# Context rows summed by TensorE beside the latents' heads, and the two layers of the first block in one program block

## The reference

```
first_block, for each of 2 layers l:
    h = rmsnorm(x, norm_mix[l]);  proj = h @ w_in[l]
    x = x + concat(mlstm, moba, nsa)(proj) @ w_out[l]
    h = rmsnorm(x, norm_ffn[l])
    x = x + square(relu(h @ w_ff1[l])) @ w_ff2[l]

second_block, latents x (256 tokens) and context xc (256 tokens), for i in 0, 1:
    attention of x over keys and values of x and xc;  x = x + g1 * (o @ w_o[i])
    the same for xc over its own keys (only i = 0)
    x = x + g2 * peer_ffn(h2, ...);   xc = xc + cg2 * peer_ffn(h2c, ...)  (only i = 0)

peer_block:  for each token 8 heads x 16 experts out of 16384 are picked:
    act = gelu(sum_d u_tab[expert] * h)          (a dot product with a gathered row u)
    out = sum over the 128 picks of g * act * v_tab[expert]   (a weighted sum of gathered rows v)
```

## Time and profile before

| | |
|---|---|
| median of 3 runs | 3413.68 us (3407.22 to 3416.61) |
| profiled execution, its own time | 3419.62 us |
| its span | 3417.8 us |
| PE / PEld / DVE / ACT / POOL busy | 2513.3 / 1409.4 / 2169.2 / 457.4 / 1318.3 us |
| HBM read | 1040.23 MB, 305 GB/s over the span |
| mean granted TensorE clock | 0.859 |

### The profile page before, as it was taken

One profiled execution on the slowest core, in us unless ns is written; L12 is line 12 of the kernel. 1 busy time (PEld: TensorE's weight loads), 2 busy tenths in 40 slices (PEclk: granted clock), 3 DMA queues, 4 the chain that ended last, 5 costly groups with the idle time before them and its releaser, 6 DMA issues. The chain is left out here.

```text
span 3417.8 us, 25077 instructions
## 1 busy us (share of the span) xinstructions
PE 2513.3 (74%) x7868; PEld 1409.4 (41%) x7868; DVE 2169.2 (63%) x5160; ACT 457.4 (13%) x1350; POOL 1318.3 (39%) x1084
## 2 busy tenths in 40 slices
PE   5786196599959469972567888887866768888876
PEld 2343154377345448431434333343333433333332
DVE  1439745856656766657867767777526377777774
ACT  0210011100002100000111111111112111111111
POOL 0000023645634555634734445454300054444442
PEclk8888597599979579986678999999988889999998
DMA  6655264789977689977858999999850199999996
GB/s 252 250 201 196 85 233 154 271 330 393 349 260 258 217 281 390 391 297 285 277 166 330 419 417 419 419 421 421 372 195 25 43 401 419 419 419 421 421 421 286
DMA packets 248920, 1044.63 MB, mean 306 GB/s; under 512 B 20518, under 2 KB 53398, under 8 KB 176852
## 3 DMA queue, kind: packets, MB, share of 16 engines
q0 software_dynamic: 147456, 805.37, 59.6%
q1 hardware_dynamic: 93584, 222.23, 17.6%
q10 hardware_dynamic: 7748, 15.43, 1.3%
HBM read 1040.23 MB, written 2.72 MB: 305 GB/s over the span
## 5 line engine op out<-in xcount | busy, mean ns | idle before, releaser
L1173 POOL DMA_INDIRECT sb_beside_slots<-in_peer_uv,sb_beside_chosen x512 | 591.6, 1156 | 616.9 <-issue 308.5
L1146 DVE SCALAR_TENSOR_TENSOR sb_beside_slots<-sb_beside_slots,sb_beside_H 128x1024 f32<-128x1024 f32 x256 | 312.7, 1223 | 236.9 <-DMA sb_beside_slots<-in_peer_uv,sb_beside_chosen 234.9
L1165 DVE SCALAR_TENSOR_TENSOR sb_xc<-sb_beside_slots,sb_beside_small,sb_xc 128x1024 f32<-128x1024 f32 x254 | 325.6, 1282 | 3.5 <-DMA sb_beside_slots<-in_peer_uv,sb_beside_chosen 1.5
L174 PE MATMUL psum<-sb_f_arena,sb_f_ring 128*128 128x256 f32 (+1 forms) x1344 | 297.6, 385 | 5.5 <-issue 5.5
L174 PEld LDWEIGHTS psum<-sb_f_arena,sb_f_ring 128*128 128x128 f32 (+1 forms) x1344 | 252.8, 189 | 50.1 <-issue 7.6
L174 PE MATMUL psum<-sb_f_ring,sb_f_arena 128*128 128x512 f32 (+2 forms) x448 | 195.6, 599 | 5.7 <-DVE sb_f_arena L1672 5.7
L1079 PE MATMUL psum<-sb_latents_ring,sb_latents_scores 128*128 128x512 f32 x304 | 147.8, 638 | 48.4 <-ACT sb_latents_scores L1037 48.4
L1079 PE MATMUL psum<-sb_last_ring,sb_last_scores 128*128 128x512 f32 x276 | 135.5, 640 | 51.2 <-ACT sb_last_scores L1037 51.2
L1079 PE MATMUL psum<-sb_beside_slots,sb_latents_scores 128*128 128x512 f32 x288 | 145.2, 652 | 30.8 <-ACT sb_latents_scores L1037 30.8
L1915 PE MATMUL psum<-sb_f_ring,sb_f_arena 128*128 128x512 f32 x384 | 165.1, 592 | 0.0
L935 POOL DMA_INDIRECT sb_latents_ring<-in_peer_uv,sb_latents_scores x76 | 91.9, 1209 | 127.1 <-PE psum L1079 86.8
(11 more groups left out here) (494 smaller groups left out, 4738.4 us busy)
## 6 DMA issues: line engine op xcount, KB each, us to landing
sb_f_ring<-in_w_ff SPq DMA_DIRECT2D x32, 2048.0 KB, 12.8
sb_context_ring<-in_ada_w SPq DMA_DIRECT2D x24, 2048.0 KB, 9.5
sb_f_ring<-in_w_in SPq DMA_DIRECT2D x8, 2048.0 KB, 12.8
sb_f_ring<-in_w_in SPq DMA_DIRECT2D x6, 1904.0 KB, 17.3
sb_context_ring<-in_peer_w_q SPq DMA_DIRECT2D x8, 1024.0 KB, 7.8
sb_beside_slots<-in_peer_uv,sb_beside_chosen POOLq DMA_INDIRECT x512, 6.4
sb_f_ring<-in_w_out SPq DMA_DIRECT2D x4, 2048.0 KB, 8.0
sb_latents_ring<-in_peer_w_q SPq DMA_DIRECT2D x8, 1024.0 KB, 25.4
```

What stands on the lines that cost most here:

```text
L174: last = e.matmul(out, a, b, start=(i == 0), stop=(i == len(terms) - 1))
L1146: e.scalar_tensor_tensor(out=self.u_slot[s % 4], in0=self.u_slot[s % 4], scalar=1.0, in1=self.H[:, s // (PH * TOPK), :], op0=ALU.mult, op1 ...
L1165: e.scalar_tensor_tensor(out=acc, in0=row, scalar=wn, in1=acc, op0=ALU.mult, op1=ALU.add).then_inc(self.added, 1)
L1173: return e.indirect_dma_start(out=to, out_offset=None, in_=self.table, in_offset=bass.IndirectOffsetOnAxis(ap=at, axis=0), element_offset= ...
```

## The change

Five things are changed together.

1. In the latents' head loop the rows n = 200 to 245 are no longer added by VectorE. ScalarE writes a diagonal of each row's weight (a 128x128 copy of the identity with the weight as scale), and TensorE multiplies it with the gathered row into two spare PSUM banks (two matmuls of 512 columns). `added` is counted up by TensorE for these rows. There are four diagonals. VectorE adds the two banks to `xc` behind the head loop, and TensorE waits for that (`joined`) before it transposes the heads' outputs.
2. Ten of the 22 steps ahead of the heads move into the head loop: 12 are left, and turns 4 to 13 of the loop take 3 steps, the others 2.
3. The two layers of the first block become one program block: one order of PSUM tiles, one weight ring that runs on, no barrier and no clearing between them. The parameters of layer 1 are loaded during the feed-forward part of layer 0 and turned between its chunks 2 and 3.
4. x is put into the feed-forward accumulator by TensorE (four matmuls with the identity), and ScalarE takes square and copy of the finished banks straight from PSUM. Layer 0's last chunk is ordered by token tile.
5. At the start of both layers ScalarE does what VectorE did: the copies of `cols`, the normalized rows (two of 128x1024) and the copies of the transposed rows (sixteen of 128x128 in place of two of 128x1024). GpSimd computes mean square and root itself, for layer 1 behind the gathers up to step 97.

```
+    beside_rows = [3 if 4 <= i < 14 else 2 for i in range(n_heads + 2)]
+    early_rows = 12
+    if beside:
+        beside.give_to_tensor(beside.at_vector + early_rows - Beside.LAG, sum(beside_rows))
...
     def scalar(e):
...
                 e.activation(pbuf[(i - 1) % 3][2][:, 0:nk], st.pair(("p", i - 1))[:, 0, 0:nk], ACT.Copy).then_inc(*st.empties(("p", i - 1)))
+            if beside:
+                beside.scalar(e, sb["weighed"], beside_rows[i])
...
     def vector(e):
...
-        more(22)
+        more(early_rows)
...
         for i in range(n_heads + 2):
-            more(2)
+            more(beside_rows[i])
...
+        if beside:
+            beside.summed(e, beside_banks)
...
     def tensor(e):
...
                 matmuls(e, st.pair(("o", j))[:, 0, 0:HD2], [...]).then_inc(st.mm, 1)
+            if beside:
+                beside.tensor(e, sb["weighed"], beside_banks, beside_rows[i])
...
+        if beside:
+            e.wait_ge(beside.joined, 2)

 class Beside, vector():
-            if n >= 0:
+            if n >= 0 and not self.on_tensor[0] <= n < self.on_tensor[1]:
...
+    def scalar(self, e, diag, rows):
+        for n in range(self.n_diag, min(self.n_diag + rows, self.on_tensor[1])):
+            e.wait_ge(self.w_ready, n // ROWS + 1)
+            if n >= self.on_tensor[0] + 4:
+                e.wait_ge(self.added, n - 3)
+            e.activation(diag[:, n % 4, :], self.C("ident"), ACT.Copy, scale=...w(n)...).then_inc(self.diag_ready, 1)
...
+    def tensor(self, e, diag, banks, rows):
+        first, end = self.on_tensor
+        for n in range(self.n_summed, min(self.n_summed + rows, end)):
+            e.wait_ge(self.diag_ready, n - first + 1)
+            e.wait_ge(self.v_in[n % 4], 16 * (n // 4 + 1))
+            for half in range(2):
+                done = e.matmul(banks[half], diag[:, n % 4, :], self.v_slot[n % 4][:, half * 512:(half + 1) * 512], start=(n == first), stop=(n == end - 1))
+            done.then_inc(self.added, 1)

 first_block, scalar():
+        for t in range(NT):
+            if gone:
+                e.wait_ge(*gone.st.computed(accs[t]))
+                e.activation(by_bank(hn, t), gone.st.pair(accs[t])[:, :, :], ACT.Square, accum_out=ss1[:, t:t + 1]).then_inc(sumsq, 1)
+                e.activation(by_bank(x, t), gone.st.pair(accs[t])[:, :, :], ACT.Copy).then_inc(*gone.st.empties(accs[t]))
...
+            e.activation(hn[:, t, :], x[:, t, :], ACT.Copy, scale=rs1[:, t:t + 1]).then_inc(hn_ready, 1)
...
+            for k in range(KT):
+                done = e.activation(hT[:, k, t * P:(t + 1) * P], turned[:, k, :], ACT.Copy, scale=cols[:, k, 4:5])
 first_block, vector():
-        beside.vector(e, 28 if l == 0 else 18)
-        e.wait_ge(ff2_done, 8)
-        for t, acc in enumerate(("accA", "accB")):
-            e.tensor_tensor(xv, xv, st.pair(acc)[:, :, :], ALU.add)
+        beside.vector(e, 18)
+        if not last:
+            beside.mark((l + 1, 0))
+            beside.vector(e, 10)
 first_block, gpsimd():
+        beside.gpsimd(e, beside.marks[l, 0] + 1 if gone else 0)
+        for t in range(NT):
+            e.wait_ge(sumsq, t + 1)
+            e.tensor_scalar(rs1[:, t:t + 1], ss1[:, t:t + 1], 1.0 / D, EPS, ALU.mult, ALU.add).then_inc(pool_step, 1)
+            e.wait_ge(pool_step, t + 1)
+            e.tensor_tensor(rs1[:, t:t + 1], rs1[:, t:t + 1], C("m05")[:, 0:1], ALU.pow).then_inc(rstd, 1)
 first_block, tensor():
+        for t in range(NT):
+            for half in range(2):
+                e.matmul(acc[t][:, half, :], ident, x[:, t, half * 512:(half + 1) * 512], start=True, stop=False)
...
+            if c == 3 and not last:
+                blocks[l + 1].column_group(e)
```

More of the change, by code:

```diff
@@ L398, in scalar @@
             e.wait_ge(y_ready, n_y)
-        for i in range(n_heads + 1):
+        for i in range(n_heads + 2):
             if i < n_heads:
@@ L1166, in vector, with give_to_tensor, summed @@
         self.at_vector = min(self.at_vector + steps, self.STEPS)
+    def give_to_tensor(self, first, count):
+        self.on_tensor = (first, first + count)
+        self.n_diag = self.n_summed = first
+    def scalar(self, e, diag, rows):
[3 more added lines that the diff above has]
+                e.wait_ge(self.added, n - 3)
+            e.activation(diag[:, n % 4, :], self.C("ident"), ACT.Copy, scale=self.buf(n // ROWS)[4][:, n % ROWS:n % ROWS + 1]).then_inc(self.diag_ready, 1)
+        self.n_diag = min(self.n_diag + rows, self.on_tensor[1])
+    def tensor(self, e, diag, banks, rows):
[6 more added lines that the diff above has]
+            done.then_inc(self.added, 1)
+        self.n_summed = min(self.n_summed + rows, end)
+    def summed(self, e, banks):
+        end = self.on_tensor[1]
+        acc = self.acc[(end - 1) // (PH * TOPK)]
+        e.wait_ge(self.added, end)
+        for half in range(2):
+            cols = slice(half * 512, (half + 1) * 512)
+            e.tensor_tensor(acc[:, cols], acc[:, cols], banks[half], ALU.add).then_inc(self.joined, 1)
+        e.wait_ge(self.joined, 2)
     def mark(self, name):
@@ L1679, in vector @@
             e.wait_ge(*st.emptied(("wo", c)))
-        norm_to_T(ss2, rs2, 2, "fT", 5)
+        e.wait_ge(sumsq, 2 * NT)
+        rms_rows(e, rs2, ss2, D).then_inc(var, 1)
+        beside.mark((l, 5))
+        e.wait_ge(rstd, 7)
+        for t in range(NT):
+            e.tensor_scalar(hn[:, t, :], x[:, t, :], rs2[:, t:t + 1], None, ALU.mult).then_inc(hn_ready, 1)
+        for t in range(NT):
+            e.wait_ge(*st.computed(("fT", t)))
+            e.tensor_tensor(hT[:, :, t * P:(t + 1) * P], flat(st.pair(("fT", t)), "p b (k n) -> p (b k) n", k=4), wide(cols[:, :, 5:6], [P, KT, P]), ALU.mult).then_inc(*st.empties(("fT", t)))
         for c in range(8):
@@ L1704, in claim @@
             return st.pair(name)
-        e.wait_ge(par, 160)
-        ps = claim("cols")
-        pc = ps[:, 0, 0:64].rearrange("p (k r) -> p k r", r=8)
-        for k in range(KT):
-            n = 7 if k < 4 else 6
-            flip(e, pc[:, k, 0:n], rows[0:n, k * P:(k + 1) * P], ident)
-        flip(e, ps[:, 0, 64:96], pe_rows[0:32, :], ident).then_inc(st.mm, 1)
+        if not gone:
+            column_group(e)
         def turned(name, turn):
@@ L1955, in layer_memory @@
     sb["slots"] = slots
+    sb["weighed"] = None if last else mem("weighed", [P, 4, P])
     return sb
@@ L2009, in build @@
                 sb = first_memory(mem(inner, "f_"))
[L2010 to L2011 removed]
+                first_blocks(nc, sems, psum, sb, A, C, x, beside)
             with ExitStack() as whole:
```

192 lines of the change are left out of this document (134 added, 58 removed).

## The result

The changed kernel takes 3547.43 us (median, 3543.86 to 3549.58); the kernel before, run beside it, takes 3413.22 us. The ratio is 1.0394, 95% interval 1.038 to 1.0408. The forecast was 3482 us, slower by 68.8; measured are 134 slower, outside its range. The profiled execution took 3549.58 us (span 3546.9), 129.96 more than that of before.

The account below looks back on a forecast made before the run. VectorE paces the head loop, its dots waiting on a chain of sums and gathers. 3419.62 + 129 - 33.6 - 30 + 3 + 0.4 = 3488.4, or +68.8; on the median, 3482.5 us, range 3425 to 3535.

Parts of the forecast that it names:

- Direction and mechanism of the loop: Head loop: gathers wait for sums behind each turn's maximum, so the loop grows by 129 us to 252.
- the upper bound: Head loop with landing 5.8, gathers at 1.5, low clock: 20.3 and 14 us a turn, 296 us, +172.
- Part 2: Ahead of the heads: ten steps fewer let the squares of q and k start earlier, gain 33.6 us.
- Part 1, the sum of a row: Head loop: a row's two matmuls on TensorE cost 0.59 + 0.43 us, 1.4 with diagonal and hand-overs at today's clock.
- R + 3.9: Head loop: R is the start of a turn's maximum; the first v gather was put 3.9 us behind it.
- rival (b): Head loop: TensorE falls to its low clock, every sum takes 1.9 us; 3510 to 3530 us, chance 12%.
- Part 1, the landing: Head loop: a turn's third u row lands 5.0 us after issue, since fewer bytes are under way.
- Parts 3 to 5, from layer 0 to layer 1: First block: projections 38.6 us earlier, VectorE 21 plus its 12.3 us wait; gain 30 us, bounds 18 to 38.
- The -26.6 of the table: Stretch up to the latents' first squares on ScalarE: forecast difference -26.6 us.
- Parts 3 to 5, the start of layer 0: Layer 0's start: ScalarE's copies and scaling lengthen TensorE's chain by 3 us, bounds 0 to 5.
- Rival (a), bound by issue: Head loop bound by GpSimd's issue, not the chain: loop 142 us, kernel 3373 us; chance 10%.
- Rival (c): First block gives back its gain, steps and weights meeting on DMA engines, VectorE setting layer 1's end: 3512 us, 8%.

Follow-up runs that it names:

- Experiments 1 and 2: Changed kernel with diagonals made ahead of the exponentials, 3422.68 us; changed kernel with v gathers issued two rows later from the loop's first step, 3451.29 us.
- experiment 6: Changed kernel with TensorE summing only each row's left half, 3521.13 us; the same also fetching only the left half of those v rows, 3503.32 us.
- experiment 5: Changed kernel's timeline between the layers read; then joined blocks with the old head part, GpSimd issuing four more rows before layer 1's roots: 3388.1 us.
- experiment 4: Changed kernel with the head part of the kernel before (VectorE adds all rows, 22 steps early, 2 a turn): 3401.69 us, ratio 0.9945.
- Experiment 1: Changed kernel with one edit, ScalarE making each turn's diagonals ahead of the exponentials and their wait for the maximum: 3422.68 us, ratio 1.0009.

## Why the prediction was wrong

Two steps carry the miss: a row's sum and a row's landing were priced too low in the head loop (38 us), and a gain of 30 us between the layers was booked that did not come (17 us of it missing).

- **Direction and mechanism of the loop: right.** The head loop is the place, and the circle sum, v gather, u gather, dot, maximum, exponentials, diagonal is what it waits for. Experiments 1 and 2 cut it at two different links, and 125 and 96 us vanish. The turns are those of the upper bound (20.3 and 14 us a turn, 296 in all; measured 20.2, 13.7 and 290), not those of the forecast. The loop alone would have given some 3520 us, inside the range; the missing gain of the first block took the time out of it.
- **Part 2: right.** 33.6 us forecast, 33.6 measured (L540 at 1552.73, right behind the third copy's end).
- **Part 1, the sum of a row: the mis-sized term.** I priced a row at two matmuls, 0.59 and 0.43, and put the first v gather at R + 3.9. It is issued at R + 5.89 in the turn shown and at R + 6.1 in the mean of turns 5 to 13. The profile's groups show four records a row, not two (184 for the 46 rows, 92 with half sums; and in the experts' stage, which the change leaves alone and whose counts the profile of before has too, 304 for 76 rows):

```profile
L1201 PE MATMUL psum<-sb_beside_slots,sb_latents_weighed 128*128 128x512 f32 x184 | 113.3, 777 | 131.8 <-ACT sb_latents_weighed L1192 131.7
L1093 PE MATMUL psum<-sb_latents_ring,sb_latents_scores 128*128 128x512 f32 x304 | 152.6, 655 | 52.1 <-ACT sb_latents_scores L1051 52.1
...
L949 POOL DMA_INDIRECT sb_latents_ring<-in_peer_uv,sb_latents_scores x76 | 92.5, 1217 | 129.8 <-PE psum L1093 89.5
```

  I took one instruction for one pass. Besides, the first row meets the low clock: its weight loads are 0.85 us apart and from 1668.4 on 0.43. In these two stretches of the turn the granted clock is 0.50 and 1.00 (columns as in the windows above):

```profile
1664.10:1668.20 4.10, 4.04 (x5) 1.85 (x6) 0.00 (x0) 0.59 (x3) 0.00 (x0) 0.50 0.02 6
1668.20:1671.00 2.80, 2.80 (x8) 1.16 (x7) 0.00 (x0) 0.00 (x0) 2.18 (x3) 1.00 0.36 83
```

  That was rival (b) in part. Half a sum less gave 1.7 us a turn back (experiment 6).
- **Part 1, the landing: the second such term.** 5.0 forecast, 5.3 for the first and 6.04 for the third u row of the turn shown. I argued that fewer bytes are under way; in the mean that holds (149 GB/s), but within a burst of six gathers it doesn't. Experiment 6 shows the bytes in it. By the rule of the Trainium skill that the forecast weighed (SBUF — State Buffer, "The DMA setup-cost knee") it would have been an estimated 3.2 us; the trace, with 5.26 to 6.09, disagrees more than I had it.
- Together: 2.9 us in each of nine turns of three steps (26), 2.0 in three turns of two (6), 4.5 in the two transitions and 2.4 in turn 15, less some 0.5 at the two ends, make the 38 us by which 290.3 exceeds 252. Of the 2.9, the sum is 2.2 and the landing 0.9, less 0.3 on the gathers and power operations between them.
- **Parts 3 to 5, from layer 0 to layer 1: the failed step.** The starts came as forecast (projections 945.1 for 946.5, dot of step 98 at 944.0 for 943.5, convolution 977.9 for 974). What failed is the step from VectorE's 12.3 us at L1467 to a gain of 12 us there: I took them for time by which TensorE was late, and so for time that an earlier start of the projections would give back. The projection that VectorE waits for stands behind a product of VectorE's own scan, as TensorE's 21.8 us wait for L1594 and the rows of experiment 5 show; only 1.5 us of it were TensorE's lateness, and the wait stayed at 12.6. The gain was therefore VectorE's 17 us alone (I had 21 for it), and some 8 of it ran out on the way: 17.2 at the convolution, 18.9 at the product L1917, 17.2 again at L1611, 11.8 at the addition of the output projection, 10.5 at the end of the second feed-forward product. Two pieces are traced. The product takes 3.75 us in place of 1.99, at a granted clock of 0.50 behind TensorE's long stop where it was 1.00 before. And the four matmuls of x take 3.4 us (eight records, the same error) in place of the 1.7 that the forecast had. The rest stays open. The -26.6 of the table became -9.4 in this execution and -15 in the medians of experiment 4; the bounds for this gain, 18 to 38 us, did not hold it.
- **Parts 3 to 5, the start of layer 0:** 3 us forecast, 0.7 measured. From the turning of the parameter rows to the projections it is 9.05 us (421.31 to 430.36) against 8.34 in the earlier trace rows; the turning itself comes 0.8 later because in this execution the whole stage starts 2.6 us later. Sixteen copies take 4.23 us, 0.26 each, not 0.39. The Trainium skill's estimate of 0.25 us for 128 columns from PSUM (VectorE: DVE Perf Modes, TRN2 errata) fits the trace better than my row from SBUF.
- **Rival (a), bound by issue:** it was described as what happens when the sums of a turn come ahead of its maximum. Experiment 1 is that kernel, and its loop is 164.7 us and not 142. Rival (c), the first block gives all back, did not happen in full: a third to a half of the 30 us was left. But its statement that VectorE sets layer 1 is what experiment 5 showed; whether rows and weights meet on the DMA engines there was not tested. Of the total of +61 us over the forecast in the profiled executions, the loop is 38, the first block 17 and the rest of the span 5.

## What to carry to other kernels

Before an operation is moved to an idle engine, write down what stands ahead of it in that engine's stream, and who waits for its result; here 59 us of VectorE's work was saved and the loop grew by 167 us, and one call, moved from the end of the loop's body to its start, took 125 of it back. Count a matmul's price from the records of the trace per unit of work, not from instructions in the source. And before a wait is booked as a gain, above all one whose releaser the profile calls "issue", read what ends it in the other engines' rows and follow that back: here it led to the waiting engine itself.

## What the runs showed of the hardware

- A float32 matmul instruction of 128x512 leaves two records, 0.43 us apart at the full clock and 0.85 at the low one (184 records for 92 instructions, 92 for the 46 of the half sums); so a row of 1024 columns costs 1.7 us on TensorE at the full clock where VectorE's addition takes 1.28.
- In the turn shown TensorE stood still for 10.6 us, then ran at the level of 1.2 GHz (granted clock 0.50, weight loads 0.85 us apart) until about 1668, and then at 2.4 GHz (1.00, 0.43). In all fifteen turns the loads of the first row's matmuls are, from the second on, 0.85 us apart, and that is the row others wait for, though the mean granted clock of the loop is 0.74.
- The second and third u row of the burst shown land 6.09 and 6.04 us after their issue where the first takes 5.26, with the DMA engines at a share of 0.44 over the loop. Halving every second row of the burst took 0.7 us off a turn.
- ScalarE copies 128 columns from PSUM in 0.26 us with a scale per partition, 16 in 4.23 us.
